# Gate columns beside the v tiles, the gate rows' chain in the second v pair, and the mixer's first chunk between the last five projection slots

## The reference, cut to what matters

```
qk = silu(causal_conv4(qk_raw));  u = conv_val * sigmoid(conv_gate)
y_conv = silu(group_norm(causal_conv31(u)))
per chunk of 128 tokens (16 chunks), per head (4):
  rows over tokens: b = cumsum(log_sigmoid(f)), running maxima m, exponents from i, b, m
  P = (q k^T) * exp(D - m_row);  num = w_inter * q C + P v;  den likewise
  h = num / max(|den|, exp(-m_row));  C = decay * C + (exp(g - m_new) k)^T v
y_mlstm = sigmoid(o) * normalise(h) * w
x = x + rms_norm([y_mlstm, y_conv] @ w_out);  then a squared-ReLU MLP of width 4096
```

## Time and profile before

| | |
|---|---|
| median of 3 runs | 2148.07 us (2147.55 to 2150.31) |
| the profiled execution | 2149.32 us, span 2147.5 us |
| PE busy | 2090.3 us, 97% of the span |
| DVE, ACT, POOL busy | 67%, 42%, 19% |
| mean granted clock of TensorE | 0.994 |
| DMA | 339 MB, 158 GB/s over the span |

### The profile page before, as it was taken

The page is one execution under the profiler, slowest core; times in us unless marked ns, Lnnn a source line. Parts: engine busy times, 40 slices in busy tenths (PEclk is TensorE's granted clock), DMA queues, the critical chain, the costliest instruction groups (busy, mean ns, idle before and its releaser), DMA issues. The chain is left out here.

```text
span 2147.5 us, 27070 instructions
## 1 busy us (share of the span) xinstructions
PE 2090.3 (97%) x10177; PEld 1752.4 (82%) x10177; DVE 1441.8 (67%) x1965; ACT 903.3 (42%) x1512; POOL 416.3 (19%) x254
## 2 busy tenths in 40 slices
PE   7999999999979999999999999999999999999998
PEld 5897878888978888778888778888888888888886
DVE  6797999889157777776666866666654536534276
ACT  5532434234344544655544644455423313313153
POOL 0000000000010231243332332233172144400012
PEclk9999999999999999999999999999999999999999
DMA  5021212112174686664455655544875454443375
GB/s 198 25 89 47 67 40 84 55 40 81 55 271 154 223 270 222 210 199 141 139 159 181 227 161 162 162 147 125 280 253 222 142 230 172 175 176 138 137 253 207
DMA packets 253520, 339.18 MB, mean 158 GB/s; under 512 B 11536, under 2 KB 196112, under 8 KB 239568
## 3 DMA queue, kind: packets, MB, share of 16 engines
q1 hardware_dynamic: 219344, 316.29, 43.9%
q10 hardware_dynamic: 33728, 21.04, 3.1%
q0 software_dynamic: 320, 0.13, 0.0%
HBM read 226.14 MB, written 111.28 MB: 157 GB/s over the span
## 5 line engine op out<-in xcount | busy, mean ns | idle before, releaser
L1651 PE MATMUL psum<-x_hi,w_hi_P 128*128 128x512 f32 x896 | 351.6, 392 | 13.1 <-DVE x_lo L1595 8.9
L1855 PE MATMUL psum<-w_hi,hid_hi 128*128 128x512 f32 x896 | 349.3, 390 | 1.9 <-DVE hid_lo L1745 1.9
L1651 PE MATMUL psum<-x_hi,w_lo_P 128*128 128x512 f32 x896 | 350.4, 391 | 0.0
L1651 PE MATMUL psum<-x_lo,w_hi_P 128*128 128x512 f32 x896 | 350.2, 391 | 0.0
L1855 PE MATMUL psum<-w_lo,hid_hi 128*128 128x512 f32 x896 | 349.1, 390 | 0.0
L1855 PE MATMUL psum<-w_hi,hid_lo 128*128 128x512 f32 x896 | 349.1, 390 | 0.0
L1745 DVE TENSOR_TENSOR hid_lo<-hid_raw,hid_hi 128x1024 fp32r<-128x1024 f32 x112 | 182.1, 1663 | 202.4 <-ACT hid_hi L1740 202.4
L1564 POOL TENSOR_TENSOR w_raw<-w_raw 128x512 f32<-128x512 f32 x128 | 179.7, 1427 | 409.6 <-DVE w_lo_P L1577 391.6
L1740 ACT ACTIVATE hid_hi<-hid_raw 128x1024 fp32r<-128x1024 f32 x112 | 112.9, 1051 | 341.5 <-DMA hid_raw<-scratch_hid 341.5
L1577 DVE TENSOR_TENSOR w_lo_P<-w_raw,w_hi_P 128x512 fp32r<-128x512 f32 x224 | 182.4, 826 | 109.1 <-ACT w_hi_P L1573 106.0
L1573 ACT ACTIVATE w_hi_P<-w_raw 128x512 fp32r<-128x512 f32 x224 | 136.7, 627 | 255.0 <-PE psum L1651 254.8
(11 more groups left out here) (241 smaller groups left out, 3895.4 us busy)
## 6 DMA issues: line engine op xcount, KB each, us to landing
scratch_hid<-stage SPq DMA_DIRECT2D x224, 256.0 KB, 3.7
hid_raw<-scratch_hid SPq DMA_DIRECT2D x56, 1024.0 KB, 4.9
w_raw<-in_w SPq DMA_DIRECT2D x52, 1024.0 KB, 5.1
w_grain<-in_w SPq DMA_DIRECT2D x48, 512.0 KB, 4.9
x_raw<-scratch_h2s SPq DMA_DIRECT2D x14, 1024.0 KB, 7.5
w_raw<-in_w_in SPq DMA_DIRECT2D x25, 512.0 KB, 3.6
scratch_h2s<-h2s SPq DMA_DIRECT2D x8, 1280.0 KB, 9.2
scratch_qk<-qout ACTq DMA_DIRECT2D x16, 512.0 KB, 3.1
```

The costliest lines, as they stand in the source:

```text
L1651: mm = nc.tensor.matmul(psum[:, bank_1(op, g), :], l, r, start=kt == 0 and i == 0, stop=kt == 3 and i == 2)
L1855: mm = nc.tensor.matmul(psum[:, bank, :], l, r, start=f == 0 and k == 0, stop=f == NFP - 1 and k == 2)
```

## The change

1. The four gates slots go. The eight gate columns (`GATE_COLS`) stand beside v pair 0's 256, so that its 8 slots x 48 = 384 matmuls are 264 columns wide. The pair is laid out by k-tiles instead of by column tiles and comes in two halves; PE waits for the second half only at its fifth k-tile. Each such slot uses two banks, and ACT copies the gate columns to `gates_c` before it evacuates v.
2. PE transposes `gates_c` to rows (`gates_t`), and the rows' chain runs in pieces at given slots from the second v pair on: PE at `ROWS_SLOT` (56) + 1, 6, 11, 12, 17; ACT at + 2, 11, 16, each between two table loads; DVE at + 3, 7, 12, 18. No store and load of the gates.
3. Both o pairs are resident in the last slots: three slots of each pair for chunks 0 to 5, then ten `ow` slots, one chunk each against all four o tiles: 24 matmuls of 512 columns. The program has 96 slots.
4. From slot 54 on slots use four banks, and the last five alternate between banks 0 and 1. Slot 90 and slot 91 both use bank 0.
5. Chunk 0's steps, and the first ones of chunk 1, stand between the last five slots (91 to 95) on PE, ACT and DVE; POOL's `qs_c` of both as well. w_out is split in slots 92 to 95, and project(0, 0) waits for its split k-tile by k-tile. Unit 7's norm steps come sooner after its taps (`LAST_UNIT_AT`).
6. SP issues chunk 0's and 1's loads as buffers come free, then w_out, then after the last slot chunk 2.

The functions of the chunk themselves (`numerators`, `weigh` and so on) do what they did.

```diff
-         + [("gates", 0, tb) for tb in range(NTB)] + pair_slots("o", 0) + pair_slots("o", 1))
+         + [("o", pair, m) for pair in range(2) for m in range(O_PAIRS)] + [("ow", 0, c) for c in range(2 * O_PAIRS, NCH)])
...
+def banks_of(s):
+
+    if s >= CHUNK_0_SLOT:
+        return [(s - CHUNK_0_SLOT) % 2]
+    if s >= ROWS_SLOT - 2:
+        return [(s - ROWS_SLOT + 2) % 4]
+    at = s + sum(with_gates(slot) for slot in SLOTS[:s])
+    return [(at + k) % 6 for k in range(2 if with_gates(SLOTS[s]) else 1)]
...
+LAST_UNIT_AT = {AT_MEAN: 0, AT_CENTER: 0, AT_SQUARE: 0, AT_VAR: 1, AT_RSTD: 1, AT_NORM: 1, AT_SILU: 1}
...
+WO_SPLITS = {CHUNK_0_SLOT + 1: (0,), CHUNK_0_SLOT + 2: (1, 2, 3), CHUNK_0_SLOT + 3: (4,), CHUNK_0_SLOT + 4: (5, 6, 7)}
...
+                    for k in range(2):
+                        o = psum[:, banks[k], 0:VG]
+                        for kt in range(KT):
+                            if k == 0 and kt == KT // 2:
+                                pe.wait_ge(sem["w_hi"], tile[1] + 1)
+                                pe.wait_ge(sem["w_lo"], tile[1] + 1)
+                            hi, lo = tokens(h_hi, kt, (2 * tb + k) * P, P), tokens(h_lo, kt, (2 * tb + k) * P, P)
+                            pairs = [(hi, vg_hi[:, kt]), (hi, vg_lo[:, kt]), (lo, vg_hi[:, kt])]
...
+                if s == ROWS_SLOT + 1:
+                    pe.wait_ge(sem["evac"]["act"], evacs(ROWS_SLOT - 1, "act"))
+                    tail["gates"](pe)
...
+                if s == CHUNK_0_SLOT:
                     pe.wait_ge(sem["c_rstd"], 2 * N_UNITS)
...
+                    scores(0)
+                if s == CHUNK_0_SLOT + 1:
+                    pe.wait_ge(sem["evac"]["act"], evacs(CHUNK_0_SLOT - 1, "act"))
+                    pe.wait_ge(sem["cols_done"], 2)
+                    numerators(0)
+                if s == CHUNK_0_SLOT + 3:
+                    transpose_y(0)
+                    scores(1)
...
+                if s == CHUNK_0_SLOT:
+                    act.wait_ge(sem["cols_done"], 2)
+                    tail["weights"](act, 0)
+                    first["wk"](0)
+                if s == CHUNK_0_SLOT + 1:
+                    first["yc_high"](0)
+                    nc.scalar.preload_act_table_set(LN_EXP)
+                    first["denominators"](0)
+                    first["head_roots"](0)
+                    nc.scalar.preload_act_table_set(EXP_TANH)
+                if s == CHUNK_0_SLOT + 3:
+                    first["y_high"](0)
+                    tail["weights"](act, 1)
+                    first["wk"](1)
+                for kt in WO_SPLITS.get(s, ()):
+                    tail["split_wo"](act, kt)
...
+                if s == CHUNK_0_SLOT - 1:
+                    first["exponents_0"]()
+                if s == CHUNK_0_SLOT:
+                    first["weigh"](0)
+                if s == CHUNK_0_SLOT + 1:
+                    first["yc_low"](0)
+                    first["update_state"](0)
+                    first["normalise_heads"](0)
+                    first["exponents"](1)
+                if s == CHUNK_0_SLOT + 3:
+                    first["y_low"](0)
+                    first["weigh"](1)
+                tail["wo_low"](dve, WO_SPLITS.get(s, ()))
...
+            def load_first():
+
+                sp.wait_ge(sem["q_out"], 16 * 16)
...
+                for c in range(2):
+                    sp.dma_start(q_t[c], dram["qk"][0, c]).then_inc(sem["chunk_in"][c], 16)
+                    sp.dma_start(v_c[c][:, :, 0:HD], by_head(dram["v"][c])).then_inc(sem["chunk_in"][c], 16)
+                    sp.dma_start(o_c[c], dram["o"][c]).then_inc(sem["chunk_in"][c], 16)
+                sp.wait_ge(sem["tap"], DVE_TAPS * N_UNITS)
+                sp.wait_ge(sem["rows_out"], 2 * H * 16)
+                for c in range(2):
+                    load_rows(c)
+                sp.wait_ge(sem["c_norm"], N_UNITS)
+                for c in range(2):
+                    sp.dma_start(k_t[c], dram["qk"][1, c]).then_inc(sem["chunk_in"][c], 16)
+                for b in range(2):
+                    sp.wait_ge(sem["c_out"][b], 16 * (N_UNITS // 2))
+                for c in range(2):
+                    sp.dma_start(yc_c[c], dram["yc"][c]).then_inc(sem["chunk_in"][c], 16)
+                load_w_out(sp)
```

More of the change, by code:

```diff
@@ L79, in tiles_of, with with_gates, o_slot @@
     kind, n, _ = slot
+    if kind == "ow":
+        return [TILES.index(("o", k)) for k in range(W_RING)]
     return [TILES.index(t) for t in ([(kind, 2 * n), (kind, 2 * n + 1)] if kind in ("v", "o") else [(kind, n)])]
+def with_gates(slot):
+    return slot[:2] == ("v", 0)
+def o_slot(c):
+    return SLOTS.index(("o", 1, c // 2) if c < 2 * O_PAIRS else ("ow", 0, c))
 def first_use(tile):
@@ L184, in th_uses @@
 def th_uses(s):
-    return sum(k in ("gate", "gates", "v", "o") for k, _, _ in SLOTS[: s + 1])
+    return sum(k in ("gate", "v", "o", "ow") for k, _, _ in SLOTS[: s + 1])
 def th_stores(s, parity):
@@ L322, in slot @@
                 tile = tiles_of(SLOTS[s])
[L323 to L329, removed]
-                r = RING[tile[0]]
-                if kind in ("v", "o"):
+                banks = banks_of(s)
+                out = psum[:, banks[0], :]
@@ L356, in group_sum @@
                                  start=True, stop=True).then_inc(sem["ln_sum"], 1)
+            scores, numerators, transpose_y = tail["tensor"](pe)[:3]
             sum_squares(0)
@@ L1162, in transpose_h2, with tensor @@
                         mm.then_inc(sem["h2_t"], 1)
-            for e in ("act", "dve"):
-                pe.wait_ge(sem["evac"][e], evacs(N_SLOTS - 1, e))
-            pe.wait_ge(sem["cols_done"], 2)
-            scores(0)
-            for c in range(NCH + 3):
+            return scores, numerators, transpose_y, project, transpose_h2
+        def tensor(pe):
+            scores, numerators, transpose_y, project, transpose_h2 = tensor_parts(pe)
+            for c in range(1, NCH + 3):
                 if c < NCH:
@@ L2105, in tile @@
         return a[:, n * P:(n + 1) * P]
-    gate_tile = np.zeros((D, P), w.dtype)
-    gate_tile[:, 0:H] = gates[:, 0:H]
-    gate_tile[:, 32:32 + H] = gates[:, H:]
     columns = {"gate": gate, "val": val, "qk": qk, "v": v, "o": o}
-    tiles = [gate_tile if kind == "gates" else tile(columns[kind], n) for kind, n in TILES]
+    tiles = [tile(columns[TILES[t][0]], TILES[t][1]) for t in W_IN_TILES]
+    gated = np.concatenate([v[:, 0:2 * P], gates], axis=1)
     params_a = np.concatenate([
```

437 lines of the change are left out of this document (262 added, 175 removed).

## The result

The changed kernel takes 2115.63 us (2112.17 to 2117.41, four runs), the kernel before 2147.81 on the same chip: 0.9846 of it, between 0.9829 and 0.9863. The forecast was 2111.8, in a range of 2107 to 2120. The profiled execution took 2116.66 us, its span is 2114.9 against 2147.5.

A forecast was written before the change was run, and what follows sets the result against it. PE, busy 97% of the span, was taken as the bound. Terms -21.76 - 3.20 + 0.3 + 0 - 1.55 - 10.1 = -36.3 us, from 2148.07, gave 2111.8 us; 8 in 10 between 2107 and 2120.

The forecast's parts named there:

- carry_in: PE's stop ahead of carry_in goes, as four or more slots lie between each step and its reader: -1.55 us.
- the last taps: Unit 7's last tap on DVE ends about 540.6, needed at slot 87's end, 543.4: 2.8 us of cover, cost 0.
- The gates slots: Removing 4 x 24 matmuls of 512 columns on PE, 0.2267 us each, saves 21.76 us.
- The 264 columns: 384 matmuls get 8 columns more, priced on the straight line between 256 and 512 columns: 1.28 us added.
- Rival D: Slots 16 to 23: 264-column matmuls run off the line between 256 and 512, costing 84 us, 2196 in all; chance 0.04.
- The ow slots: Ten slots of 24 matmuls, 5.44 us each in place of 5.76: -3.20 us.
- Slot 16: Twelve matmuls ahead of PE's wait gain 1.5 us, paying for the wide columns; both together 0; remaining stop under 0.5 us.
- Slot 91: It takes slot 90's bank, so PE waits for the evacuation: cost 0.84 us.
- yc of chunk 0: Loaded by F + 24.5 (F: slot 87's end), ahead of scores(0) at F + 26.0: 1.5 us of cover, hidden.
- rival A: First chunk late, its waits between slots: yc of chunk 0, DVE's last tap or ACT's evacuations; up to 2121.9 us; chance 0.18.
- y(1): Behind the last slot y(1) comes at E + 12.9 (E: that slot's end), so transpose_y(1) waits 1.6 us.
- rival C: Clock falls between or behind the slots at short PE stops, about 3.5 us more, 2115; chance 0.04 beyond the forecast's range.

The follow-up runs named there:

- four slots more: The changed kernel with slot 79's 24 matmuls done five times instead of once: 2138.73 us, 0.9940 of the kernel before.
- the other bank: The changed kernel with the last five slots on banks 1, 0, 1, 0, 1 instead of 0, 1, 0, 1, 0: 2114.01 us, 0.9837 of the kernel before.
- unit 7 later: The changed kernel with unit 7's mean, squares, variance and root taken one slot later: 2115.59 us, 0.9843 of the kernel before.

## Why the prediction was right, step by step

The sum said -36.3 us up to numerators(2); measured are -32.6, and -34.1 in the execution without the fall of the clock. The main terms, the removed slots, the wider ones, carry_in and the work moved out of the seam, did what the sum said. One cost that was put at nothing was there (the last taps), the clock fell in one of two traced executions, and some sizes were off. The measured time lies 3.8 us above the forecast, and this is not all of the error: the wide columns, priced 1.0 us too high, hid that much of the taps' 1.4 by luck.

- **The gates slots**, 21.76: right, the run with four slots more gives 21.17 plus 0.59 taken up by a stop.
- **The 264 columns**, 1.28: too much. Over 381 starts the wide matmuls stand 0.1208 us apart, against 0.1200 at 256 columns: 384 of them cost 0.3 us, not on the straight line. Rival D had no part. Its price of 84 us was misread besides: 0.66 us is the length of a row of the plain fp32 sums with the pass through the pipeline, while their starts are 0.43 us apart (four take 1.88 us, one alone 0.59), which makes 264 columns 0.22 us and the price 38.
- **The ow slots**, 3.2: 2.8 by the eight measured.
- **Slot 16**: twelve matmuls come ahead of the wait and leave a stop of 0.36 us, under the 0.5 forecast. **carry_in**: no stop. **Slot 91**: a stop of 0.78 for 0.84, which cost 1.05 by the run with the other bank. **scores(2)**: 1.82 for 1.8.
- **The last taps**: the step that failed. I gave them 2.8 us of cover; PE stood for 1.44. The slots' side was right within 0.8 us (542.6 for 543.4), VectorE's last tap ended at 544.03 in place of 540.6. I had counted the instructions that VectorE gets, and for its waits "two short idles" of before. Before, these two were 0.30 and 0.16 us. In the changed kernel it waits three times for ScalarE in that stretch, 2.22, 0.65 and 1.68 us, 4.55 where I had put nothing. The other two parts were smaller than I counted: the work added was 1.75 us for 1.95, and the stretch started 0.35 late for 1.3. The first row of it:

```profile
482.12 3.92 DVE L761 SCALAR_TENSOR_TENSOR qout<-qraw,par_a,qout 128x1024 f32<-128x1024 f32 x3 [2.22 <-ACT qout L567]
```

  The timeline of all engines in the changed kernel ahead of it shows whom ScalarE waited for: the store of the qout before, issued at 475.39, right behind eight stores of the rows by GpSimd that the change moved to this place.

```profile
472.76 2.12 POOL L963 DMA_DIRECT2D scratch_rows<-neg_m  x4 [470.75 <-DVE inter L1073]
...
474.86 1.92 POOL L963 DMA_DIRECT2D scratch_rows<-inter  x4
475.39 0.37 ACTq L576 DMA_DIRECT2D scratch_qk<-qout  x1
...
480.93 1.15 ACT L567 ACTIVATE qout<-qraw,par_a 128x1024 f32<-128x1024 f32 x1 [5.58 <-DMA scratch_qk<-qout]
```

  Before, the same store held ScalarE 3.35 us, with the DMA engines busy 0.49 of 475 to 481; in the changed kernel 5.58, with 0.67. What made it late stays open. The rows' stores stand right ahead of it, but they moved only 0.06 MB of the 1.12 in these 6 us, and no run moved them alone. A rival: the load of a weight tile, 512 KB, was issued closer ahead of this store, at 472.02 and 3.4 us ahead, before at 471.11 and 3.8 us ahead. In the last 1.9 us of the wait hardly anything moved, as the window of the changed kernel shows (length, busy times, clock, DMA share, GB/s): a share of 0.07 is about one DMA engine of the 16.

```profile
479.00:481.00 2.00, 2.00 (x11) 1.65 (x10) 0.90 (x1) 0.07 (x1) 0.00 (x0) 1.00 0.07 19
```

  The other two waits, 2.33 us together, don't come from a late store: ScalarE's stops at the next two stores are 3.06 and 3.05 us, before 3.07 and 3.66. There VectorE and ScalarE only meet in another order, which I hadn't followed. I had priced the moved chain's instructions, and neither its DMAs nor what its place does to the turns of the two engines.
- **yc of chunk 0** had 5.1 us of cover (here at 565.4, scores(0) at 570.53) where I counted 1.5. Of rival A only the part on VectorE's last tap came true, and for 1.44 us.
- **y(1)**: transpose_y(1) waited 2.54 for 1.6. The 1.1 us that VectorE's product spent beside GpSimd's account for this; with that product moved transpose_y(1) waited 1.28.
- **The clock**: I forecast no fall in the likeliest case (rival C); it fell in the profiled execution and cost 1.64 us, and did not in the second one. The Trainium skill, page "TensorE: Matmul & The Clock Gate", section "A second HAM failure mode: psum-queue depth-cycling", tells of another kernel, in which frequent short idles between groups of matmuls bring it. The trace agrees that stops much shorter than the 4.80 us of the earlier trace rows can be enough, and shows that they often aren't.

Added up: -36.3 + 1.4 (taps) + 0.9 (y(1)) + 1.6 (clock) - 1.0 (wide columns) + 0.4 (ow) + 0.2 (slot 91) = -32.8, for -32.6 measured.

## What to carry to other kernels

When a chain of small steps is moved in front of a busy stretch, follow the engines' waits for each other through that stretch, and the DMAs that they wait for, and don't carry over the idle times of before: here 0.46 us of them became 4.55, and a matmul 40 to 60 us later waited. Work that stood in a seam is worth moving between slots even at no fewer instructions: it gave 7.5 us here by the times, 9.8 by the traces. And a stop that is taken out of a chain in which three engines take turns comes back where the next of them is late (1.44 us became 1.93, 1.81 became 2.20), so look for the next one before the edit, not behind it.

## What the hardware showed that I had not expected

- A VectorE product of 128 by 4 takes 0.16 us alone and up to 1.25 beside a GpSimd product that started ahead of it, and ends with it: 608.24 + 1.25 and 608.20 + 1.27; in the run with unit 7 later 609.43 + 0.62 and 608.76 + 1.26. Larger operations meet it too: VectorE's four exponents of chunk 0 took 2.18 us beside GpSimd's product (at 565.46), where a later chunk's four take 1.13. The Trainium skill, page "SBUF — State Buffer", section "Who interferes with whom", has a VectorE instruction with two inputs in SBUF contend with a GpSimd instruction that reads SBUF, and calls the ports that they share an exclusive lock. The trace agrees.
- Matmuls of 264 columns run at the rate of 256 (0.1208 and 0.1200 us), not 0.0033 slower.
- The granted clock fell to its lower level for 3.3 to 3.4 us behind single stops of 1.88, 1.93, 1.96 and 2.20 us and within one of 2.74 (slot 16 waiting for both tiles), and for 6.7 us behind one of 2.29 (four slots more); in the changed kernel it fell only 1.4 us behind the end of a stop of 2.54. It did not fall at others of 1.99, 2.27 and 2.74, nor in the second execution of one and the same program. What decides it stays open. Its price was 1.6 us where PE was busy all through it (the changed kernel, slot 91 with unit 7 later), and less where a stop lay in it.
